# Expert-choice norms: squares and roots in the stage in front, scaling by two engines, two halves, other ring slots

## What is computed

```python
def moe_ec(h, router_w, w1, w3, w2):
    b, T, _ = h.shape
    cap = EC_CAPACITY * T // N_EXPERTS_2
    logits = jnp.einsum('btd,de->bte', h, router_w, preferred_element_type=jnp.float32)
    aff = jax.nn.softmax(logits, axis=-1)
    gate, idx = lax.top_k(jnp.swapaxes(aff, 1, 2), cap)
    xg = h[bidx, idx]
    a = jnp.einsum('becd,edf->becf', xg, w1)
    g = jnp.einsum('becd,edf->becf', xg, w3)
    y = jnp.einsum('becf,efd->becd', jax.nn.silu(a) * g, w2)
...
    x = x + g2l * moe_ec(rmsnorm(x, norm2_w[i]) * (1.0 + sc2l) + sh2l, ...)
    if not last:
        ctx = ctx + g2c * moe_ec(rmsnorm(ctx, norm2_w[i]) * (1.0 + sc2c) + sh2c, ...)
```

## Time and profile before

| | us |
|---|---|
| median of three runs | 2229.8 |
| the runs | 2228.2, 2229.8, 2230.95 |
| the profiled execution | 2231.04 |
| its span, first to last instruction | 2229.2 |
| TensorE busy | 2030.7 (91%) |
| VectorE busy | 972.8 (44%) |
| ScalarE busy | 648.5 (29%) |
| GpSimd busy | 72.4 (3%) |

### The profile page before, as it was taken

How to read it: one execution, slowest core, us unless ns; L and a number is a source line. 1 busy time by engine, 2 the same in 40 slices (tenths; PEclk the granted TensorE clock), 3 DMA queues, 4 the chain that set the end, 5 groups by cost and what they waited for, 6 DMA issues and landing times. The chain is left out here.

```text
span 2229.2 us, 25119 instructions
## 1 busy us (share of the span) xinstructions
PE 2030.7 (91%) x10198; PEld 1076.0 (48%) x10198; DVE 972.8 (44%) x1668; ACT 648.5 (29%) x1284; POOL 72.4 (3%) x106
## 2 busy tenths in 40 slices
PE   6987988999899999999899999988899899999887
PEld 5844444444377888878643333322445422222222
DVE  4687224444688889882522221222466400011002
ACT  4244023111276667762211111100226111111000
POOL 0101010000000000000100000000120000000000
PEclk9999998999999999999999999999999999999999
DMA  8637477899333433322489999999820599999997
GB/s 289 214 139 277 176 266 294 339 388 384 111 97 98 139 105 114 114 96 77 186 360 429 427 428 427 427 428 428 328 110 1 211 427 427 424 427 426 427 425 301
DMA packets 147177, 623.58 MB, mean 280 GB/s; under 512 B 15443, under 2 KB 66134, under 8 KB 109046
## 3 DMA queue, kind: packets, MB, share of 16 engines
q1 hardware_dynamic: 142144, 601.65, 67.8%
q0 software_dynamic: 2352, 16.91, 1.9%
q10 hardware_dynamic: 2566, 3.41, 0.5%
HBM read 620.76 MB, written 1.18 MB: 279 GB/s over the span
## 5 line engine op out<-in xcount | busy, mean ns | idle before, releaser
L2898 PE MATMUL bank<-slots,xgTe 128*64 128x512 f32 (+1 forms) x1584 | 355.0, 595 | 30.4 <-DMA slots<-in_moe_w 30.3
L3119 DVE TENSOR_TENSOR actse<-sge,bank 32x512 f32<-32x512 f32 (+1 forms) x48 | 32.8, 682 | 499.2 <-PE bank L2898 278.4
L2898 PEld LDWEIGHTS bank<-slots,xgTe 128*64 128x64 f32 (+1 forms) x1584 | 102.7, 125 | 259.5 <-issue 216.2
L2898 PE MATMUL bank<-slots,aTe 128*64 128x512 f32 (+1 forms) x800 | 188.4, 615 | 18.3 <-issue 18.3
L514 PE MATMUL bank<-slots_r 128*128 128x512 f32 x512 | 201.2, 393 | 0.0
L3016 ACT ACTIVATE sge<-bank 32x512 f32<-32x512 f32 (+1 forms) x48 | 28.3, 590 | 481.5 <-PE bank L2898 481.3
L513 PE MATMUL bank<-hT_r,slots_r 128*128 128x512 f32 x384 | 155.6, 405 | 0.0
L515 PE MATMUL bank<-slots_r 128*128 128x512 f32 x384 | 152.0, 396 | 0.0
L583 PE MATMUL bank<-slots,hT 128*128 128x512 f32 (+1 forms) x320 | 133.2, 578 | 4.6 <-DVE hT L480 3.0
L2898 PEld LDWEIGHTS bank<-slots,aTe 128*64 128x64 f32 (+1 forms) x800 | 55.3, 128 | 130.8 <-issue 130.8
L514 PEld LDWEIGHTS bank<-slots_r 128*128 128x128 f32 x512 | 96.3, 188 | 22.6
(11 more groups left out here) (561 smaller groups left out, 3099.0 us busy)
## 6 DMA issues: line engine op xcount, KB each, us to landing
slots<-in_moe_w SPq DMA_DIRECT2D x149, 2048.0 KB, 26.5
slots<-in_ada_w SPq DMA_DIRECT2D x24, 2048.0 KB, 12.2
extra0e<-in_moe_w SPq DMA_DIRECT2D x23, 2048.0 KB, 26.5
slots<-in_ssd_in_w SPq DMA_DIRECT2D x48, 512.0 KB, 5.3
slots<-in_moe_w_gate SPq DMA_DIRECT2D x23, 1024.0 KB, 10.6
slots<-in_moe_w_up SPq DMA_DIRECT2D x23, 1024.0 KB, 12.6
slots<-in_moe_w_down SPq DMA_DIRECT2D x23, 1024.0 KB, 7.3
rowsB<-acum_rows POOLq DMA_DIRECT2D x16, 1024.0 KB, 5.8
```

Source lines behind the costliest of these rows:

```text
L2898: i = pe.matmul(bank[64 * n:64 * n + NJ * CAP, :], lhsT(4 * h + k), wv[:, 0, n * 512:(n + 1) * 512], start=(h == 0 and k == 0), stop=(h == ...
L3119: i = dve.tensor_tensor(acts[r_, :], sg[r_, :], psum[1][r_, :], ALU.mult)
```

## The change

- **Squares and roots in the stage in front.** At the end of the SSD stage ACT waits for each tile's last addition (`stream_added`), squares it, and POOL makes the root (`early_squares`, `early_roots`); likewise at the end of the attention stage for the two tiles of `X`. The root has a third POOL operation, which takes over a factor that VectorE's scaling had. The stage of the mixture has neither squares nor roots.
- **Scaling by two engines.** Of each pair of tiles VectorE scales the first, ACT the second (`shared_scale`); TensorE waits for one or the other (`wait_normed`).
- **The norm in halves.** Layer 0's norm of four tiles becomes two of two tiles. A bank then holds two chunks of two tiles. Layer 1's norm has two tiles as before.
- **Slots.** The scratch in slots 4 and 5 of the ring is given back with the evacuation of the last group's y (`group_scratch`), slot 3 with the last `sum_squares` (`gate_scratch`), slots 0 to 2 at the end (`end_scratch`). For that `y_high` moves into `h_high`, `rowsB` and `hT`. Layer 0's pieces go into the slots in the order 5, 4, 3, 0, 1, 2, extra; the qkv and output weights and layer 1's order follow it. Layer 1 gets `queries_slot` with `C` in place of `extra1` with `C`: the memory of the attention's queries `q`, free when they have been transposed (`queries_room`), and this piece is the fifth of nine instead of the eighth.
- The additions to `X` in the attention stage lose a wait of VectorE for itself.

```diff
-        scratch_use = Piece(None, None, 0, None)
+        group_scratch, gate_scratch, end_scratch = (Piece(None, None, 0, None) for _ in range(3))
         for slot in range(SLOTS):
-            ring.last[slot] = scratch_use
+            ring.last[slot] = (end_scratch, end_scratch, end_scratch, gate_scratch, group_scratch, group_scratch)[slot]
...
-        moe2_weights(0, (0, 1, 2, 3, 4, 5, SLOTS))
-        ring.last[SLOTS + 1] = ring.last[SLOTS + 2] = extra_room[1]
+        moe2_weights(0, (5, 4, 3, 0, 1, 2, SLOTS))
+        ring.last[SLOTS + 1] = extra_room[1]
         ring.last[SLOTS + 3] = extra_room[2]
         for n in (0, 1, 2):
-            weights(("qkv", n), [(0, KD, 512, rows("attn_qkv_w_2")[:, :, n * 512:(n + 1) * 512])], (n + 5) % SLOTS)
+            weights(("qkv", n), [(0, KD, 512, rows("attn_qkv_w_2")[:, :, n * 512:(n + 1) * 512])], (2, 5, 4)[n])
         for n in range(2):
-            weights(("attn_out", n), [(0, 4, D, rows("attn_out_w_2")[:, 4 * n:4 * n + 4, :])])
-        moe2_weights(1, (4, 5, 0, 1, 2, 3, SLOTS + 1, SLOTS + 2, SLOTS + 3))
+            weights(("attn_out", n), [(0, 4, D, rows("attn_out_w_2")[:, 4 * n:4 * n + 4, :])], (3, 0)[n])
+        queries_room = Piece(None, None, 0, None)
+        ring.last[SLOTS + 2] = queries_room
+        moe2_weights(1, (1, 2, 5, 4, SLOTS + 2, 3, 0, SLOTS + 1, SLOTS + 3))
...
+
+        def stream_root(pool, t, done):
+
+            link = chain(pool, pool_step)
+            c = slice(t, t + 1)
+            link(pool.tensor_scalar(rstd[:, c], eps_rows[:, c], float(D * EPS), None, ALU.add))
+            link(pool.tensor_tensor(rstd[:, c], rstd[:, c], minus_half[:, 0:1], ALU.pow))
+            pool.tensor_scalar(rstd[:, c], rstd[:, c], float(D) ** 0.5, None, ALU.mult).then_inc(done, 1)
+
+        def early_squares(act, junk, tiles):
+
+            for t, src in enumerate(tiles):
+                act.wait_ge(stream_added, counted["added"] + 1)
+                if t:
+                    act.wait_ge(squared, counted["streams"] + t)
+                counted["added"] += 1
+                act.activation(junk, src, ACT.Square, accum_out=eps_rows[:, t:t + 1]).then_inc(squared, 1)
+
+        def early_roots(pool, n):
+
+            for t in range(n):
+                pool.wait_ge(squared, counted["streams"] + t + 1)
+                stream_root(pool, t, rooted)
...
+            def shared_scale(self, eng, by):
+                for t, src in enumerate(self.srcs):
+                    if (t % 2 == 0) != (by == DVE):
+                        continue
+                    eng.wait_ge(rooted, self.before + t + 1)
+                    dst = self.xn[:, t, :].rearrange("p (h j m) -> p h m j", h=2, j=4)
+                    src = src.rearrange("p (h m j) -> p h m j", h=2, j=4)
+                    r = rstd[:, self.at + t:self.at + t + 1]
+                    if by == DVE:
+                        eng.tensor_scalar(dst, src, r, None, ALU.mult).then_inc(normed, 1)
+                    else:
+                        eng.activation(dst, src, ACT.Copy, scale=r).then_inc(act_normed, 1)
+
+            def wait_normed(self, pe, t):
+                if not self.shared:
+                    pe.wait_ge(normed, self.before_dve + t + 1)
+                elif t % 2 == 0:
+                    pe.wait_ge(normed, self.before_dve + t // 2 + 1)
+                else:
+                    pe.wait_ge(act_normed, self.before_act + t // 2 + 1)
...
-            pos[0] = late + 2080
-            y_high_late = carve(8 * 512, flat_r).rearrange("p (c n) -> p c n", c=8)
-            y_high = lambda i: h_high[:, i, :] if i < 8 else y_high_late[:, i - 8, :]
+            y_high = lambda i: (h_high[:, i, :] if i < 4 else rowsB_r[:, 1, i - 4, :] if i < 8
+                                else hT_r[:, i - 8, :])
             ssum = w_dt[:, :, :].rearrange("p k n -> p (k n)")
             assert pos[0] <= SLOTS * SLOT
             rows_flat = rowsB[:, :, :, :].rearrange("p d h n -> p (d h n)")
             g1 = rows_flat[:, 0:2048].rearrange("p (s n) -> p s n", s=2)
+            junk = hp[:, :, :, :].rearrange("p a b n -> p (a b n)")[:, 0:D]
...
+                group_scratch.freed = (emptied[DVE], banks["y", SSD_G - 1, 1].done)
                 sum_squares(6)
                 gate_banks(pe, "g1", 0, 2, 0, ACTE)
                 gate_banks(pe, "g1", 0, 2, 1, ACTE)
                 sum_squares(7)
+                gate_scratch.freed = (bank_full, banks["ss", 7].full)
...
-                scratch_use.freed = (bank_full, b.full)
+                end_scratch.freed = (bank_full, b.full)
...
+                early_roots(pool, TT)
...
+                early_squares(act, junk, streams)
...
-                        dve.tensor_tensor(streams[t][:, c], streams[t][:, c], p_, ALU.add)
+                        i = dve.tensor_tensor(streams[t][:, c], streams[t][:, c], p_, ALU.add)
+                    i.then_inc(stream_added, 1)
...
-                if l == 0:
-                    segs = mod_segments(0, 1)
-                else:
-                    segs = lambda k: [(0, S, ncol[:, 1, 1, 0, k:k + 1], modcol[:, 1, 6 + k // 4, k % 4, 0:1])]
-                norm = NormT(tag, [r for rs in res for r in rs], xn, hT, segs, apart=True)
+                def segs_of(j):
+                    return lambda k: [(0, S, ncol[:, l, 1, sid[j], k:k + 1], modcol[:, l, 6 + k // 4, k % 4, sid[j]:sid[j] + 1])]
+
+                norms = [NormT(f"{tag}s{j}", res[j], xn[:, NT * j:NT * (j + 1), :], hT[:, :, S * j:S * (j + 1)], segs_of(j),
+                               at=NT * j, shared=True) for j in range(NJ)]
...
-                    if l == 0 and n % 7 == 6 or l == 1 and n % 9 == 6:
+                    if l == 0 and n % 7 == 6 or l == 1 and n % 9 == 7:
                         piece.ap = extra[0][:, :]
-                    if l == 1 and n % 9 == 7:
-                        piece.ap = extra[1][:, :]
+                    if l == 1 and n % 9 == 4:
+                        piece.ap = early_at[1][:, :]
                         piece.second = C[:, :, :].rearrange("p t d -> p (t d)")
                     if l == 1 and n % 9 == 8:
                         piece.ap, piece.second = extra[2][:, :], hflat[:, 2048:4096]
...
                     if l == 1:
                         hold(pe, 4)
-                    norm.tensor(pe)
+                    for norm in norms:
+                        norm.tensor(pe)
...
                     for k in range(KD):
-                        norm.wait_chunk(pe, k)
+                        for norm in norms:
+                            norm.wait_chunk(pe, k)
...
-                    norm.pool(pool)
...
-                    norm.scalar_squares(act)
-                    norm.evacuate(act, ACTE)
+                    for norm in norms:
+                        norm.shared_scale(act, ACTE)
+                    for norm in norms:
+                        norm.evacuate(act, ACTE)
...
-                    norm.vector_scale(dve)
-                    norm.evacuate(dve, DVE)
+                    for norm in norms:
+                        norm.shared_scale(dve, DVE)
+                    for norm in norms:
+                        norm.evacuate(dve, DVE)
...
+            queries_at = (nc.sbuf_base + 31) // 32 * 32
+            q = sb("q5", [P, NT, QH * 64], scope=scope)
+            early = ring["moe2", 1, 4]
+            queries_slot = nc.alloc_sbuf_tensor_at("queries_slot", [P, SLOT // 2], F32, offset=queries_at)
+            early_at.extend((queries_at, queries_slot[:, :]))
+            early.ap, early.second = queries_slot[:, :], C[:, :, :].rearrange("p t d -> p (t d)")
...
+                queries_room.freed = (bank_full, banks["qT5", to_qT.groups()[-1][0]].full)
...
+                early_roots(pool, NT)
...
+                early_squares(act, probs[:, 0:2, :].rearrange("p a n -> p (a n)"), X_tiles)
...
-                        link(dve.tensor_tensor(X[:, t, c], X[:, t, c], part[:, n, :], ALU.add))
+                        i = dve.tensor_tensor(X[:, t, c], X[:, t, c], part[:, n, :], ALU.add)
+                    i.then_inc(stream_added, 1)
```

22 lines of the change are left out of this document (17 added, 5 removed).

## The result

| | before | after |
|---|---|---|
| median of 20 runs each, same chips, us | 2230.07 | 2235.44 |
| lowest and highest | 2226.85, 2236.94 | 2229.54, 2241.5 |
| ratio | | 1.0026 [1.0018, 1.0034] |
| profiled execution, us | 2231.04 | 2235.24 |
| its span, us | 2229.2 | 2233.4 |

The ratio's interval is above 1, so the change is slower by about 0.26%. The forecast was 2229.6 with a range up to 2233.0, so the time lies outside it. The two expert-choice layers still run at 427 GB/s, as before. In the clock row the last slice is 8, where before has 9.

A forecast was written before the change was run, and what follows sets the result against it. The prediction took the two expert-choice layers' DMA stream at 427 GB/s, started by the first slot given back, as the bound. Layer 0 -3.4 and layer 1 +3.2 sum to -0.2 us, median 2229.6, range 2225.3 to 2233.0.

The forecast's parts named there:

- What bounds the kernel, and the early slots: Both expert-choice layers: the 427 GB/s DMA stream bounds; earlier transfers only lengthen the holes before it, 0 us.
- First slot given back, plus a fixed stream: Each expert-choice layer ends a fixed stream time after its first slot is given back; 87 pieces, 427 us after the second hole.
- C: Rival: transfers given early count in full, 19.6 us gone, 2210.2; one piece gives some 5 us, 2224.7; chance 0.07.
- SP's side effect: Layer 0's opening: with three issues left instead of six, SP ends near 1092.7 and holds nobody.
- Layer 0: Layer 0's norm: opening 1.0 us later, but transposes and halved evacuation end sooner; -3.4 us.
- The bound of -1.5 for layer 0: Layer 0's norm: if the evacuation's overlap failed, 1.9 us are lost and -1.5 remain.
- ACT's scaling: Layer 0's second tile: even at twice the square's 1.06 us, ACT is done in time and nobody waits.
- D: Rival: ACT scales slowly in layer 0; at 4 us a tile 1.8 us are lost, sum +1.6, 2231.4; chance 0.12.
- Layer 1: Layer 1's norm: opening 2.5 us later uncovers the filler, +1.4; at half clock the filler takes 1.85 more, +3.2 us.
- From then on the stream does not break: After each layer's first give-back the DMA stream runs without a hole, 4.9 us a piece.
- E: Rival: TensorE stays at 1.2 GHz up to layer 1's first expert, router and gather double; +5.3, 2235.1; chance 0.07.
- The bound of the range: Worst case: layer 0 at -1.5, layer 1 at +3.2, one more half-rate stretch of 1.85; 2233.3, cut to 2233.0.

The follow-up runs named there:

- the four slow kernels: The changed kernel, e2, e4, and the new slots alone with layer 1's opening delayed on purpose; medians 4 to 6 us above before.
- e2: The changed kernel with the slots as before, so the new norms only; median 2234.3 us, ratio 1.0016 to the kernel before.
- e6: The changed kernel with four fillers at the attention stage's end and two instead of four at layer 1's head; 2230.7 us, ratio 0.9998 to before.
- e8: The changed kernel without the filler at layer 1's head; median 2231.4 us, ratio 1.0003 to the kernel before.
- e4: The changed kernel run once more, for a second trace; median 2235.7 us, ratio 1.0023 to the kernel before.

## Why the prediction was wrong, point by point

**What bounds the kernel, and the early slots: right.** Both holes are there and longer, and e1 with the new slots alone gives 0.9998. In front of layer 0 the transfers end at about 1112 in after, where they ended at about 1126, and nothing is lost by it. *First slot given back, plus a fixed stream* holds in part: layer 1's first give-back sets the four slow kernels (32.2 to 32.4 us) apart from all others (27.6 to 29.4), but the stream is not fixed (422.8 to 425.3). The gain of 19.6 us (C) or a part of it can't be seen in the medians.

**SP's side effect: right**, and worth 1.6 us of layer 0's opening (e1: 0.28 after the last addition, before: 1.88). It is most of what layer 0 gains up to the gather. Counted from the last addition to the start of the gather, before has 28.4 us, e1 26.8, after 26.5.

**Layer 0: right in sign, too large by 1.4 us** (-2.0 for -3.4), and the failed term is the opening. The head of layer 0 of after, in order of time:

```profile
1091.62 0.69 DVE L2791 TENSOR_TENSOR X<-X,xst 128x512 f32<-128x512 f32 x1
...
1092.34 1.06 ACT L376 ACTIVATE hp<-X 128x1024 f32<-128x1024 f32 x1 [1.63 <-DVE X L2791]
...
1094.52 0.23 POOL L367 TENSOR_SCALAR rstd<-rstd 128x1 f32<-128x1 f32 x1
...
1096.50 2.08 ACT L481 ACTIVATE xne<-C,rstd 128x1024 f32<-128x1024 f32 x1 [3.01 <-PEq L2101]
...
1098.32 5.23 PE L513 MATMUL bank<-consts,xne 128*128 128x128 f32 x32 [7.53 <-DVE xne L479]
1104.07 2.37 PE L2899 MATMUL bank<-hT,actse 128*32 128x512 f32 x16 [0.53 <-DVE hT L535]
```

The square, the root and its third operation took what the sum said: from the last addition's end (1092.31) to POOL's end (1094.75) are 2.44 us, the sum had 2.49. But from there to the opening (1096.47) are 1.72 us, where I had put 0.43 from SP's end to the first square. The opening is 4.16 after the last addition, not 2.9. The transposes started 1.85 us after it (2.0 predicted) and took 5.23 (5.15 predicted). The halves did their part: the router's matmuls, which had waited for one chunk after the other for 3.81 us, take 2.37. But the late opening eats all but 0.3 us of it (26.8 against 26.5), and more where the clock is worse: in e2, e6 and e8 all 32 transposes ran at half rate (in e6 the granted clock was 0.50 from 1100 to 1104), took 6.6 us instead of 5.23, and the gather started after 27.9. The row of e6:

```profile
1099.90 6.64 PE L513 MATMUL bank<-consts,xne 128*128 128x128 f32 x32 [7.56 <-DVE xne L479]
```

So up to the gather the new norm of layer 0 gives 0.3 us against e1 or costs 1.1, as the clock falls. The bound of -1.5 for layer 0 took a failure of the overlap, not this.

**ACT's scaling: right.** It takes 2.08 us a tile, twice the square's 1.06, and nobody waits for it (D is out).

**Layer 1: the mechanism of the forecast was right up to the filler, and the cost behind it was left out.** The opening came 2.27 us later (2.5 predicted), the filler was uncovered and took 5.25 (5.5 predicted), so the gather started 2.7 us later than before, counted from the last addition (3.2 predicted). The step that failed stands in "From then on the stream does not break" and in the sum: I let the half rate end with the filler. The gather went at half rate too (+1.5, hence +4.25 at the first give-back), one more stretch delayed the fifth piece and the stream (+1.7), and one fell behind the stream (+1.7): 7.6 us in all, where the sum had +3.2. This is what E was about, with the wrong place: E had the clock low without a break up to the first expert, with the router at 3.4 us. The router took 1.68. The clock came back, and fell again behind short idle times of TensorE that the kernel before has too, and without a fall. E's 2235.1 lies near the measured 2235.4, partly by luck: of its +5.5 for router and gather only 1.5 is there, and 3.4 come from behind the first expert, which E didn't name. I gave E 0.07 since near 1101.8 the clock had come back after 3.7 us of work; that row says that it comes back, not that it stays.

**The bound of the range.** It had one more half-rate stretch of 1.85 us beside its worst case, and was cut to 2233.0. Three fell in after, each at 1.5 to 1.7 us.

**What stays open:** why the half rate returns 15 us after the first give-back and at the very end of after. In e4 and e8 the last piece of the span is 29.1 and 29.2 us long too, in e2 27.4. And I can't say what GpSimd does in the 1.72 us between its last operation and the opening at the end of the SSD stage.

## What to carry over

Moving work in front of a stage's opening takes it off one path and puts it on another: the opening waits for it, and every engine with it. When TensorE is the engine that then stands still, price its clock too, and allow for more half-rate stretches than the one in the next instructions. Filler belongs into the idle time itself, where it did not delay the opening (e6, 2.78 against 2.76 us), and not behind it, where it stands in the queue ahead of real work (after, 5.25 us). Move only the work that ends before the stage would open anyway: with the last tile's square and root left behind the opening (e5) the loss was gone. None of the kernels here is faster than the one before beyond the noise.
